# A different order of work at the entries of six stages of a two-block transformer kernel

## What is computed

```python
# first block (layer norms between the parts, residual factor ALPHA)
y = hgrn2_mixer(h);            h = ln(ALPHA * h + y)
y = swiglu(h);                 h = ln(ALPHA * h + y)   # 1024 -> 2816 -> 1024
y = diff_attention_mixer(h);   h = ln(ALPHA * h + y)   # w_in is 1024 x 3072
y = moe_swiglu(h);             h = ln(ALPHA * h + y)   # 8 experts, 1024 -> 3584 -> 1024, top 2
# second block (rms norms)
h = h + conformer_conv(rmsnorm(h))                     # w_pw1 is 1024 x 2048
h = h + square(relu(rmsnorm(h) @ w1)) @ w2             # 1024 -> 4096 -> 1024
h = h + sigmoid(rmsnorm(h) @ w_gate) * (p @ w_proj)
k, v, c = shared_kv(h); h = h + fox_attention(rmsnorm(h), k, v, c)
h = h + square(relu(rmsnorm(h) @ w1)) @ w2;  h = h + sigmoid(...) * (...);  return rmsnorm(h)
```

## Time and profile before

| What | Value |
|---|---|
| Median of 3 runs | 2544.25 us (2544.16 to 2549.97) |
| Profiled execution, its own time | 2540.45 us |
| Its span | 2538.6 us |
| TensorE matmul busy | 2383.9 us, 94% of the span |
| VectorE busy | 1789.2 us, 70% |
| ScalarE busy | 1464.9 us, 58% |
| Mean granted TensorE clock | 0.977 of full |

### The profile page before, as it was taken

One profiled execution on the slowest core, in us unless ns is written; L12 is line 12 of the kernel. 1 busy time (PEld: TensorE's weight loads), 2 busy tenths in 40 slices (PEclk: granted clock), 3 DMA queues, 4 the chain that ended last, 5 costly groups with the idle time before them and its releaser, 6 DMA issues.

```text
span 2538.6 us, 29790 instructions
## 1 busy us (share of the span) xinstructions
PE 2383.9 (94%) x11221; PEld 1966.1 (77%) x11221; DVE 1789.2 (70%) x1680; ACT 1464.9 (58%) x1562; POOL 56.7 (2%) x99
## 2 busy tenths in 40 slices
PE   7888999887999999999999999997889999889997
PEld 5677788676788888888888888886777887777886
DVE  5675554675889898989898988887765455554454
ACT  4522444363777777777777777775574446455444
POOL 0000000002200000000000000000010000000000
PEclk9999999998999999999999999998999999999999
DMA  7203554404999999999999999995403545413542
GB/s 294 104 5 117 183 193 165 172 34 153 363 333 388 326 384 331 377 337 379 335 378 336 372 342 377 340 372 198 141 4 133 199 168 180 144 68 133 197 157 78
DMA packets 264116, 589.69 MB, mean 232 GB/s; under 512 B 8417, under 2 KB 39377, under 8 KB 263760
## 3 DMA queue, kind: packets, MB, share of 16 engines
q1 hardware_dynamic: 261376, 579.38, 62.7%
q0 software_dynamic: 2608, 8.93, 1.1%
q10 hardware_dynamic: 32, 0.02, 0.0%
HBM read 587.22 MB, written 1.05 MB: 232 GB/s over the span
## 4 chain that ended last, share of the span: by engine, by line
PE 80%; DVE 9%; ACT 6%; DMA 3%; issue 2%; ACTq 0%; DVEq 0%; SPq 0%
PE up L1914 15%; PE up L1916 15%; PE up L1915 15%; PE acc L1914 8%; PE acc L1916 8%; PE acc L1915 8%; DVE wl L1296 4%; ACT wh L764 3%; PE up L2368 2%; DMA raw<-in_ffn_w 2%; PE acc L2235 1%; PE up L2131 1%; PE tp L2271 1%; PE acc L2117 1%; DMA raw<-in_hg_w_in 1%
## 5 line engine op out<-in xcount | busy, mean ns | idle before, releaser
L1603 DVE TENSOR_TENSOR wl<-raw,wh 128x2048 fp32r<-128x2048 f32 x378 | 864.8, 2291 | 127.2 <-ACT wh L984 124.3
L984 ACT ACTIVATE wh<-raw 128x2048 fp32r<-128x2048 f32 x378 | 727.1, 1924 | 226.9 <-PE up L1916 136.8
L1914 PE MATMUL up<-wh,xTh 128*128 128x512 f32 x1888 | 760.0, 403 | 45.3 <-DVE wl L1296 6.5
L1916 PE MATMUL up<-wh,xTl 128*128 128x512 f32 x1888 | 744.7, 394 | 0.0
L1915 PE MATMUL up<-wl,xTh 128*128 128x512 f32 x1888 | 743.9, 394 | 0.0
L1296 DVE TENSOR_TENSOR wl<-raw,wh 128x2048 fp32r<-128x2048 f32 x171 | 389.6, 2291 | 383.4 <-ACT wh L764 382.1
L764 ACT ACTIVATE wh<-raw 128x2048 fp32r<-128x2048 f32 x171 | 325.0, 1917 | 378.6 <-PE up L1916 208.7
L1914 PEld LDWEIGHTS up<-wh,xTh 128*128 128x128 f32 x1888 | 360.0, 191 | 128.0 <-issue 35.8
L1916 PEld LDWEIGHTS up<-wh,xTl 128*128 128x128 f32 x1888 | 359.3, 190 | 77.4
L1915 PEld LDWEIGHTS up<-wl,xTh 128*128 128x128 f32 x1888 | 360.6, 191 | 71.5 <-issue 0.7
L1914 PE MATMUL acc<-wh,hTh 128*128 128x512 f32 x848 | 330.7, 390 | 2.3 <-DVE hTl L1623 1.5
(11 more groups left out here) (360 smaller groups left out, 1950.6 us busy)
## 6 DMA issues: line engine op xcount, KB each, us to landing
raw<-in_moe_w_gate SPq DMA_DIRECT2D x126, 1024.0 KB, 6.3
raw<-in_moe_w_up SPq DMA_DIRECT2D x126, 1024.0 KB, 6.8
raw<-in_moe_w_down SPq DMA_DIRECT2D x126, 1024.0 KB, 5.8
raw<-in_ffn_w SPq DMA_DIRECT2D x32, 2048.0 KB, 8.6
raw<-in_hg_w_in SPq DMA_DIRECT2D x7, 2048.0 KB, 13.2
raw<-in_da_w_in SPq DMA_DIRECT2D x6, 2048.0 KB, 8.4
raw<-in_ffn_w_gate SPq DMA_DIRECT2D x11, 1024.0 KB, 6.9
raw<-in_ffn_w_up SPq DMA_DIRECT2D x11, 1024.0 KB, 11.0
```

Source lines behind the costliest of these rows:

```text
L984: f(wh[:, x % SPLITS, :], raw[:, x % RAW, :], ACT.Copy).then_inc(moe["hi"], 1)
L1603: V.tensor_tensor(wl[:, x % SPLITS, :], raw[:, x % RAW, :], wh[:, x % SPLITS, :].bitcast(F32), ALU.subtract).then_inc(moe["lo"], 1)
L1914: mm(out, x_hi, w_hi, start=start, stop=False)
L1916: return mm(out, x_lo, w_hi, start=False, stop=stop)
```

## The change

It reorders work and removes none.

- ScalarE and VectorE, first feed-forward only (`by_block`): in unit 0 the split that stood ahead of block 0's step stands between block 0's and block 1's.
- TensorE, all three feed-forwards: the turns of unit 0 stand inside unit 1, behind its first half.
- VectorE, differential attention: block 0 of the first unit is rotated ahead of the first split; block 1 behind it; then the two other splits.
- ScalarE, experts: the copy `y` moves from the start into the third step of the first expert, between `gate_act` and the split of the second down half.
- Convolution and key/value projection: roots (ScalarE) and reciprocals (VectorE) go ahead of the first split, and block 0's step ahead of splits; a memset on VectorE moves behind block 1's step.

```diff
@@ ScalarE, mlp @@
             for u in range(len(ts) // NB):
-                split()
+                if u > 0 or not by_block:
+                    split()
                 for b in range(NB):
+                    if u == 0 and b == 1 and by_block:
+                        split()
                     step_act(g0 + NB * u + b, half[:, b, 0:width], up[:, b, 0:width], gate,
...
-        mlp(g_ff, t_ff, ACT.Silu, HALF, 1)
+        mlp(g_ff, t_ff, ACT.Silu, HALF, 1, by_block=True)
@@ ScalarE, expert @@
                     gate_act(at, t_)
+                if t_ == 3 and before is None:
+                    f(y, h[:, :, :], ACT.Copy, scale=ALPHA).then_inc(s_y, 1)
...
         split_half(start, 0, 3)
-        f(y, h[:, :, :], ACT.Copy, scale=ALPHA).then_inc(s_y, 1)
         gate_act(start, 0)
@@ ScalarE, convolution @@
         mean_squares(H_CV)
+        row_roots(H_CV)
         split(1)
-        row_roots(H_CV)
         for c in range(4):
-            split()
             if c > 0:
+                split()
                 for b in range(NB):
                     step_copy(t_cv[NB * (c - 1) + b], uT[:, :, PADC:], c - 1, b, 2)
             for b in range(NB):
+                if c == 0 and b == 1:
+                    split()
@@ ScalarE, key/value projection @@
                 mean_squares(H_Q)
+                row_roots(H_Q)
                 split(1)
-                row_roots(H_Q)
@@ VectorE, differential attention @@
-        split(1)
         dve.wait_ge(s_cst, 16)
         for s in range(12):
             g, c, b = g_da + s, s // NB, s % NB
-            if b == 0:
+            if s == 1:
+                split(1)
+            if b == 0 and s > 0:
                 split()
...
+            if s == 1:
+                split()
             if b == NB - 1:
                 split()
@@ VectorE, convolution @@
         mean_squares(H_CV)
-        split(1)
         row_scales(H_CV)
-        link(V.memset(uT[:, :, 0:PADC], 0.0))
...
-            if b == 0:
+            if b == 0 and s > 0:
                 split()
...
             dve.sem_inc(cv_n, 1)
+            if s == 0:
+                split(1)
             wait_act()
...
             V.tensor_tensor(stage[:, g % 2, 0:HALF], hf[:, 0:HALF], hf[:, HALF:W], ALU.mult).then_inc(s_st, 1)
+            if s == 1:
+                split()
+                link(V.memset(uT[:, :, 0:PADC], 0.0))
@@ TensorE, mlp @@
+            def turns(u):
+                for b in range(NB):
+                    turn_step(g0 + NB * u + b, ts[NB * u + b], tiles)
+
             for u in range(units + 1):
...
-                    unit(g0, u, t0, order=order)
+                    unit(g0, u, t0, behind=turns if u == 1 else None, order=order)
...
-                if u < units:
-                    for b in range(NB):
-                        turn_step(g0 + NB * u + b, ts[NB * u + b], tiles)
+                if 1 <= u < units:
+                    turns(u)
```

More of the change, by code:

```diff
@@ L895, in _, with mlp @@
         layer_norms(T_ff, split)
-        def mlp(g0, ts, gate, width, down_halves, scale=None, after_turns=None):
+        def mlp(g0, ts, gate, width, down_halves, scale=None, after_turns=None, by_block=False):
             for u in range(len(ts) // NB):
-                split()
+                if u > 0 or not by_block:
+                    split()
                 for b in range(NB):
+                    if u == 0 and b == 1 and by_block:
+                        split()
                     step_act(g0 + NB * u + b, half[:, b, 0:width], up[:, b, 0:width], gate,
@@ L1443, in _, with mlp @@
         layer_norm(accb, A_HG, turned=T_ff, between=split)
-        def mlp(g0, ts, width, off, down_halves, scale=None, after_turns=None):
+        def mlp(g0, ts, width, off, down_halves, scale=None, after_turns=None, by_block=False):
             for u in range(len(ts) // NB):
-                split()
+                if u > 0 or not by_block:
+                    split()
                 for b in range(NB):
                     s = NB * u + b
+                    if u == 0 and b == 1 and by_block:
+                        split()
                     wait_act()
@@ L1488, in _ @@
             V.tensor_tensor(w_lo[:, :, :], w[:, :, :], w_hi[:, :, :].bitcast(F32), ALU.subtract).then_inc(s_wl, 1)
-        mlp(g_ff, t_ff, HALF, HALF, 1)
+        mlp(g_ff, t_ff, HALF, HALF, 1, by_block=True)
         layer_norm(accb, A_FF, turned=T_da)
         tmp = flat(half[:, :, :]).rearrange("p (i u n) -> p i u n", i=4, u=8)
-        split(1)
         dve.wait_ge(s_cst, 16)
```

## The result

The changed kernel takes 2529.02 us, the median of four runs (2527.65 to 2531.36). The kernel before, run beside it, takes 2546.93 us (four runs, 2544.16 to 2549.97). The ratio is 0.9931, with a 95% interval of 0.9918 to 0.9945: a gain of 17.9 us. The forecast was 2527.0 us, and a gain of 17.2.

A forecast was written before the change was run, and what follows sets the result against it. TensorE was taken as the bound, with 80% of the chain, so only its stops and half-clock time could go. Terms 2.7 + 7.0 + 5.1 + 4.2 - 1.0 - 0.8 = 17.2 us gave 2527 us, range 2519 to 2533.

The forecast's parts named there:

- First feed-forward: Its entry: stops of 1.4 and 1.3 us replace 3.66, and the half-clock stretch goes; gain 2.7 us.
- Differential attention: Its projection's entry: the 4.02 us stop goes and the half unit behind it returns to full speed; gain 7.0 us.
- Convolution: Its projection's entry: the 3.50 us stop goes and the half unit behind it runs 1.6 us faster; gain 5.1 us.
- Key/value projection: Its entry: a stop of 1.75 us stays for 4.30, and the half unit runs 1.7 us faster; gain 4.2 us.
- Residual copy: First expert's third step: the moved copy delays the next split and makes a new TensorE stop; loss 1.0 us.
- removing it gains 0 at the start: Experts' start: taking the 1.90 us copy away gains 0, as VectorE waited for the up products with the gate ready.
- Later turns: Both later feed-forwards: turns inside the second unit delay ScalarE's next split and the chain behind it; loss 0.4 us each.
- TensorE's stop (1.96) ends with block 0's eviction: nothing gained: Later feed-forwards: the stop ends with that eviction whether turn or matmul follows, so moving the turns gains nothing.
- the clock doesn't come back: Rival at the four entries: stops go but half-clock stretches fall elsewhere; gain 9.2 us, 2535 us; chance 0.15.
- A new wait in place of the old: Rival at the four entries: delayed splits make unit 1 wait; gain 0 to 8 us, about 2540 us; chance 0.10.
- Late loads: Rival at the four entries: SP's loads behind delayed splits arrive late; 9.8 us slower, 2554 us; chance 0.05.
- the table load: ScalarE's function switch costs 1.28 us; the skill's added drain of some 1.38 us was left out of the sum.

The follow-up runs named there:

- kernel 1: Changed kernel with unit 0's turns back ahead of unit 1 in the two later feed-forwards; 2530.57 us, ratio 0.9929 to the kernel before.
- kernel 2: Changed kernel with the residual copy back at the experts' start; 2527.34 us, ratio 0.9925 to the kernel before.
- kernel 4: Changed kernel with the copy back at the experts' start and the two later feed-forwards' turns back ahead of unit 1; 2529.52 us, ratio 0.9928.
- Experiment 5: Changed kernel with unit 0's turns ahead of unit 1 in all three feed-forwards, the first keeping its order by block; 2530.97 us, ratio 0.9958.
- kernel 3: Kernel before with only the new VectorE order in the differential attention's projection; 2540.19 us, ratio 0.9969 to the kernel before.
- Experiment 6: Changed kernel with the copy at the experts' start and, in the key/value projection, the first split ahead of the squares; 2526.6 us, ratio 0.994.
- kernel 7: Changed kernel with the copy at the experts' start and block 0's step ahead of the split in both later feed-forwards too; 2523.61 us, ratio 0.9927.
- kernel 8: Same edits as kernel 7, plus the key/value projection's first split ahead of the squares; 2519.31 us, ratio 0.9909 to the kernel before.

## Why the prediction was right

It was right in size (17.2 forecast, 17.9 measured, by its interval 14.0 to 20.9) and, by the stretches, in its terms: 19.2 from the entries, less 1.1 for the copy and some 0.8 for the turns, is 17.3. That the whole time agrees within 0.7 us is in part luck, since an interval of 7 us can't tell that, and kernels 1, 2 and 4, which by their stretches should gain 1 to 2 us more than the change, have the same ratio as it within 0.0006.

- **First feed-forward**, 2.7 forecast, 2.6 in every trace that has both edits. Two sizes were off and nearly cancelled. The second stop is 0.90 and not 1.3, since block 0's twelve matmuls took 3.0 us (272.75 to 275.77, that is 276.67 - 0.90) where the price of a full-clock step gave 2.73. The first is 1.45 for 1.4. Experiment 5 shows that block 0's matmuls must stand ahead of the turns for it. The order by block on ScalarE and VectorE is the other half; no run leaves it out of this stage alone.
- **Differential attention**, 7.0 forecast, 7.11 to 7.16 in all nine traces that have the order, one of them with this edit alone. The clock's part, forecast at 2.96, came back (8.42 to 5.50 us for the half unit).
- **Convolution**, 5.1 and 5.3. No experiment takes this part apart; kernel 3, which lacks it, has the old time there (+0.02), and the other eight the new (-5.28 to -5.32). Which of its moves pays is read from the timeline alone. **Key/value projection**, 4.2 and 4.2, with a stop of 1.65 for the forecast 1.75. Experiment 6 shows that the rest was the wait named.
- **Residual copy**, -1.0 forecast, -1.14 measured, with a stop of 0.73. The step "removing it gains 0 at the start" held too. This part of the change does harm, if little.
- **Later turns**, -0.4 in each forecast; ScalarE's split starts 0.4 later with them in every pair of traces in which the clock behaved alike (experiment 1), and unit 2 with it, give or take the half microsecond by which the time of the load behind it varies. A step that was missing is the start of unit 1: "TensorE's stop (1.96) ends with block 0's eviction: nothing gained" is so, but the trace of before showed a full clock behind that stop, and I took this as its price. In the changed kernel the clock fell there, 1.6 us, as it does with the old order in kernels 1, 3, 4 and 5.

Of the rivals, "the clock doesn't come back" is refuted at the entries: 1.00 in the windows behind all four. Its gain of 9.2 lies outside the measured interval of 14.0 to 20.9. "A new wait in place of the old" is refuted by the stretches, each of which would have gained 2.3 less; only the key/value projection has such a wait, as forecast. "Late loads" is refuted in the entries, where no ScalarE wait for a DMA appears, and by the experts behind them, unchanged but for the copy. As to the table load, the trace of after repeats it twice: 1.28 us, the next activation starts 0.01 and 0.02 us behind its end (270.48 + 1.28 against 271.77, 2145.68 + 1.28 against 2146.98), and the load itself starts 0.03 us or less behind the activation before it. The drain that the Trainium skill (ScalarE: Activation LUTs, What ACT_TABLE_LOAD costs) adds doesn't show.

What stays open: why the clock is held at half for 3 us in one execution and for 7 in another, from the same instruction on (454.91 before, 454.62 after, above), and why it falls behind some stops of 2 us and not behind others. No run here tells it.

## What to carry to other kernels

At the entry of a stage ask of each engine's list, for the eviction that frees the first bank: what stands in front of it that TensorE needs only later? Moving it forward paid 19 us here, and in the first feed-forward only where TensorE's list has that bank's work next: the two lists are changed together. Price the slow stretch behind a stop with the stop, judge an edit of a few us by the same stretch of two traces, and don't take one trace's clock behind a stop as its price.

## What the hardware showed that was not expected

- **A stop of 2 us is on the edge.** Stops of 1.95 to 2.07 us stand ahead of unit 1 of both later feed-forwards in the traces of before, after and kernels 1 to 6. Behind them the granted clock fell to half in 9 of 16 cases: neither of the two in the trace of before, one of the two in those of after and kernels 1, 2, 3 and 5, both in 4 and 6. Each fall cost 1.5 to 1.7 us. At the entries it never fell behind the stops of 1.4 and 0.9, of 1.65 and of 0.4 (nor, in kernels 7 and 8, behind the 0.20 of the later feed-forwards), and always behind those of 3.5 to 4.3, eight in number. It is no rule for other kernels, where other work stands around the stop.
- **Executions of the same kernel differ by the clock.** Four runs of the changed kernel lie within 3.7 us, those of kernel 3 within 12.2. The three fastest of kernel 3 (2534.0 to 2535.1) have a mean granted clock of 0.979, the slowest (2546.21) 0.973. Only one trace of each kernel is kept, so where one kernel's runs differ isn't shown; between kernels, the stretches that no edit touches differ by longer or shorter times at half clock (+1.16 at the attention's first unit, +0.2 to +2.9 in the first mixer). The trace of before has the shortest first mixer of all ten, in line with its time of 6.5 us under the median.
